# Other byte offsets for the on-chip arrays: the big region 128 bytes further, the split input activations 64 bytes further

## The chip, the core and the metric

The kernel runs on one core of one Trainium2 chip. Its time is device time in microseconds (us), the median of several executions; lower is better. On-chip memory (SBUF) has 128 partitions; an array that the kernel places there occupies the same byte offset in every partition, and this case is about those offsets alone. TensorE multiplies a stationary block of 128 columns, which a weight load (LDWEIGHTS) puts into the array first, by a moving block of up to 512 columns (MATMUL). Both blocks are read from SBUF.

## The reference

```python
h = rms_norm(x, norm_mix);  proj = h @ w_in          # 256 x 2048 by 2048 x 4624
out_a = sliding-window attention with sinks (16 heads, 4 key heads, rotary)
out_b = forgetting attention (16 heads)
x = x + concat(out_a, out_b) @ w_o                   # 2048 x 2048
h = rms_norm(x, norm_ffn)
u = h @ w_up                                         # 2048 x 11264
c = causal depthwise convolution of width 3 of u;  gate, val = halves of c
x = x + (silu(gate) * val) @ w_down                  # 5632 x 2048
return rms_norm(x, norm_final)
```

All is float32, for 256 tokens and one layer.

## The kernel before

Every large product is made of three. A float32 operand is split into a rounded part `hi` and a remainder `lo`, and the kernel adds hi·hi, hi·lo and lo·hi. ScalarE rounds (`split_hi`, L480; `down_hi`, L737), VectorE subtracts (`split_lo`, L793; `down_lo`, L1071), each a tile of 128 x 1024 at a time. SyncE loads the weight tiles of 512 KB into a ring of four slots, `raw`, and waits before each for `lo_done`; the halves go to the ring `split`.

The stages, in order of time:

- The first tiles (`values_and_gates`): activations `act_split` stationary, weights moving, 272 columns, three matmuls for each product (`mm3`, L1245 to L1247).
- Four passes of `quad`, for a head group each: `features` (L1257 and L1259: weights stationary, `act_split` moving, one matmul of 512 columns over hi and lo of the activations and one of 256), `tokens` (L1272 and L1274: `act_split` stationary, weights moving, 512 and 256), with the attention of the pass before between the tiles.
- The product with `w_o`: `mm3` with `mix_hi` and `mix_lo` stationary, weights of 512 columns moving.
- 22 `up_step`s (L1505 and L1507, in the form of `features`). Ahead of the first step's fourth tile stand four small matmuls on the array `diag2` (L1516), which spread the second norm's factors.
- The product with `w_down`: `mm3` with `g_hi` and `g_lo` stationary, 512 columns moving. Some tiles ("sums", one recursion of a fast product) use sums of activations instead, `s_hi` and `s_lo`, which lie in the space of `act_split`. VectorE also forms sums of weights (L1111 to L1116) for these.
- The last norm and the stores.

The arrays are placed one behind the other by a cursor. `Sbuf` starts it at the first free byte rounded up to 64, here 16512, and `place` rounds each size up to 32:

```python
        t = self.nc.alloc_sbuf_tensor_at(name, shape, dt, offset=self.cursor)
        self.cursor += (4 * int(np.prod(shape[1:])) + 31) // 32 * 32
```

A slot of the rings takes 4352 bytes, which is 8 · 512 + 256, so that neighbouring slots differ by 256 modulo 512. The offsets below are worked out from these two lines and the shapes; "modulo 512" is the offset's remainder.

| array | byte offset | modulo 512 |
|---|---|---|
| `raw`, `split` (slots 0 and 2; 1 and 3) | 16512, 33920 | 128; 384 |
| `nat` | 68736 | 128 |
| `act_split` (also `s_hi`, `s_lo`, `z_gain`) | 85120 | 128 |
| `ident`, `ones`, `cst`, `r2b`, `small` | 117888 to 121472 | 128; `small` 128 |
| region: `g_hi`, `g_lo`; in the same space `mix_hi`, `mix_lo` and the arrays of the attention | from 121856 | 0 |
| `ub`, `gfin` behind the region | 211968 | 0 |
| `conv_o`, `silu`, `up_r` | 216096 to 222240 | 32 |
| `diag2`, in the same space `t24` | 224288 | 32 |

Within an array the blocks that TensorE takes as stationary lie 512 bytes apart, so they keep the remainder. The moving blocks do too, except those of 272 columns: they lie 1088 bytes apart, 64 more modulo 512 for each next one.

Of the kernel before, what the change touches and what calls it, by code (L numbers as in the profile page):

```python
# [148 lines left out]
class Sbuf:  # L149


    def __init__(self, nc):
        self.nc, self.cursor = nc, (nc.sbuf_base + 63) // 64 * 64

    def place(self, name, shape, dt=F32):
        t = self.nc.alloc_sbuf_tensor_at(name, shape, dt, offset=self.cursor)
        self.cursor += (4 * int(np.prod(shape[1:])) + 31) // 32 * 32
        return t


def program(nc, x, norm_mix, w_in, sinks, b_f, w_o, norm_ffn, w_up, conv_w, conv_b, w_down, norm_final,
            ident_c, tri_c, mask_b_c, cos_c, sin_c, out):
    ctx = ExitStack()
    with ctx:
        sbuf = Sbuf(nc)
# [10 lines left out]
        split = sb("split", [P, 2, RING, SLOT], R32)  # L176
        hi, lo = split[:, 0], split[:, 1]
        nat = sb("nat", [P, MT, D])
        act_at = sbuf.cursor
        act_split = sb("act_split", [P, 2, KB, S], R32)  # L180
        act_hi, act_lo = act_split[:, 0], act_split[:, 1]
# [5 lines left out]
        small = sb("small", [P, 96])  # L187


        region = sbuf.cursor  # L190
        g_hi = sb("g_hi", [P, FB, S], R32)
        g_lo = sb("g_lo", [P, FB, S], R32)
# [43 lines left out]
        conv_o = sb("conv_o", [P, 2, 2, S])  # L236
        silu = sb("silu", [P, 2, S])
        up_r = sb("up_r", [P, 2, S])
        top = sbuf.cursor
        sbuf.cursor = region_end  # L240
        ysq = sb("ysq", [P, MT, 512])
# [1391 lines left out]
```

## Time and profile before

| | |
|---|---|
| median of 3 runs | 1074.91 us (1074.58 to 1075.35) |
| the profiled execution | 1073.68 us, span of its instructions 1071.9 us |
| granted TensorE clock | 0.999 of full speed |
| PE (matmuls) busy | 1060.3 us, 99% of the span |
| VectorE (DVE) busy | 803.3 us, 75% |
| ScalarE (ACT) busy | 614.1 us, 57% |
| DMA | 201.65 MB, mean 188 GB/s |

The profile has one record for each instruction. A matmul's duration in it is modelled and overlaps the next one's; what a matmul costs in a stream is read from the distance between two starts. Times in the timeline are rounded to 0.01 us, so distances are taken over several matmuls.

### The profile page before, as it was taken

How to read it: one execution, taken by the hardware profiler on the slowest of the kernel's cores; microseconds unless marked ns; L12 is line 12 of the kernel's file. 1: busy time of each engine (PE TensorE's matmuls, PEld its weight loads, DVE VectorE, ACT ScalarE, POOL GpSimd, SP SyncE). 2: the span in 40 equal slices, each digit the busy share in tenths (PEclk: the TensorE clock that was granted, in tenths of full speed). 3: DMA queues.
4: the chain of work that ended last, by engine and by line, in shares of the span. 5: the costliest groups of instructions: out<-in, count | busy, mean ns of one | idle time of the engine just before them, and what ended most of it. 6: DMA issues, size and time to landing. Idle time of an engine off the chain costs nothing.

```text
span 1071.9 us, 17534 instructions
## 1 busy us (share of the span) xinstructions
PE 1060.3 (99%) x5963; PEld 908.7 (85%) x5963; DVE 803.3 (75%) x1193; ACT 614.1 (57%) x946; POOL 9.5 (1%) x30
## 2 busy tenths in 40 slices
PE   9999999999999999999999999999999999999997
PEld 8888888888888888888888888888888788888885
DVE  5677777676565777877777777777877998887786
ACT  6957475745555655565555565555555555555553
POOL 1000000000000000000000000000000000000000
PEclk9999999999999999999999999999999999999999
DMA  9575556554555566556666566655666656556663
GB/s 298 170 235 173 174 164 176 158 175 154 180 171 183 174 199 195 181 172 202 192 197 188 167 206 191 199 180 175 199 194 194 201 193 204 189 194 202 202 198 127
DMA packets 171330, 201.65 MB, mean 188 GB/s; under 512 B 8580, under 2 KB 138340, under 8 KB 171168
## 3 DMA queue, kind: packets, MB, share of 16 engines
q1 hardware_dynamic: 170576, 199.59, 59.7%
q0 software_dynamic: 400, 1.27, 0.4%
q8 instruction: 21, 0.34, 0.1%
q10 hardware_dynamic: 320, 0.34, 0.1%
q14 instruction: 13, 0.11, 0.0%
HBM read 199.06 MB, written 2.11 MB: 188 GB/s over the span
## 4 chain that ended last, share of the span: by engine, by line
PE 97%; DVE 1%; DMA 1%; issue 0%; ACT 0%; SPq 0%; DVEq 0%; ACTq 0%
PE tr_ps L1505 15%; PE pj L1505 15%; PE pj L1257 9%; PE pj L1507 8%; PE tr_ps L1507 8%; PE pj L1245 5%; PE pj L1247 5%; PE pj L1246 5%; PE pj L1259 5%; PE sc_ps L1245 4%; PE sc_ps L1246 4%; PE sc_ps L1247 4%; PE pj L1272 3%; PE pj L1274 1%; PE tr_ps L1245 1%; PE tr_ps L1247 1%
## 5 line engine op out<-in xcount | busy, mean ns | idle before, releaser
L793 DVE TENSOR_TENSOR split<-raw,split 128x1024 fp32r<-128x1024 f32 x282 | 340.9, 1223 | 147.8 <-ACT split L480 142.3
L480 ACT ACTIVATE split<-raw 128x1024 fp32r<-128x1024 f32 x276 | 287.4, 1056 | 107.1 <-PE pj L1507 33.0
L1505 PE MATMUL tr_ps<-act_split,split 128*128 128x512 f32 x704 | 245.3, 391 | 0.0
L1505 PE MATMUL pj<-act_split,split 128*128 128x512 f32 x704 | 245.0, 391 | 0.0
L1507 PE MATMUL pj<-act_split,split 128*128 128x256 f32 x704 | 197.1, 280 | 0.0
L1507 PE MATMUL tr_ps<-act_split,split 128*128 128x256 f32 x704 | 197.1, 280 | 0.0
L1505 PEld LDWEIGHTS pj<-act_split,split 128*128 128x128 f32 x704 | 131.6, 187 | 28.9
L1505 PEld LDWEIGHTS tr_ps<-act_split,split 128*128 128x128 f32 x704 | 131.7, 187 | 28.8
L1257 PE MATMUL pj<-act_split,split 128*128 128x512 f32 x416 | 147.9, 399 | 0.0
L1507 PEld LDWEIGHTS tr_ps<-act_split,split 128*128 128x128 f32 x704 | 133.0, 189 | 0.1
L1507 PEld LDWEIGHTS pj<-act_split,split 128*128 128x128 f32 x704 | 133.1, 189 | 0.0
L1259 PE MATMUL pj<-act_split,split 128*128 128x256 f32 x416 | 116.1, 279 | 0.0
L737 ACT ACTIVATE split<-raw 128x1024 fp32r<-128x1024 f32 (+1 forms) x84 | 80.5, 984 | 34.9 <-PE sc_ps L1247 14.2
L1071 DVE TENSOR_TENSOR split<-raw,split 128x1024 fp32r<-128x1024 f32 (+1 forms) x84 | 92.2, 1131 | 4.1 <-ACT split L737 4.1
L1257 PEld LDWEIGHTS pj<-act_split,split 128*128 128x128 f32 x416 | 78.1, 188 | 18.4 <-issue 0.5
L1259 PEld LDWEIGHTS pj<-act_split,split 128*128 128x128 f32 x416 | 78.4, 188 | 0.0
L701 ACT ACTIVATE conv_o<-ub,cst 128x256 f32<-128x256 f32 x88 | 48.2, 596 | 22.2 <-DVE ub L1033 22.2
L1245 PE MATMUL sc_ps<-split,g_hi 128*128 128x512 f32 x148 | 58.6, 396 | 0.0
L1246 PE MATMUL sc_ps<-split,g_hi 128*128 128x512 f32 x148 | 58.4, 395 | 0.0
L1247 PE MATMUL sc_ps<-split,g_lo 128*128 128x512 f32 x148 | 58.4, 395 | 0.0
L737 ACT ACTIVATE split<-t 128x1024 fp32r<-128x1024 f32 x28 | 29.6, 1060 | 48.3 <-PE sc_ps L1247 27.5
L711 ACT ACTIVATE g_hi<-silu 128x256 f32 (+1 forms) x44 | 16.6, 418 | 54.7 <-DVE silu L1050 54.7
(244 smaller groups left out, 1502.5 us busy)
## 6 DMA issues: line engine op xcount, KB each, us to landing
raw<-w_up SPq DMA_DIRECT2D x176, 512.0 KB, 4.3
raw<-w_down SPq DMA_DIRECT2D x88, 512.0 KB, 4.4
raw<-w_in SPq DMA_DIRECT2D x72, 512.0 KB, 3.8
raw<-w_o SPq DMA_DIRECT2D x32, 512.0 KB, 4.3
nat<-x SPq DMA_DIRECT2D x8, 256.0 KB, 6.4
key_bias<-nft_dram SPq DMA_DIRECT2D x4, 512.0 KB, 4.8
result<-nat SPq DMA_DIRECT2D x7, 256.0 KB, 3.1
gfin<-norm_final POOLq DMA_DIRECT2D x1, 1024.0 KB, 4.8
```

Of the source, the lines that this page charges most:

```text
L480: act.activation(hi[:, slot, 0:TILE], raw[:, slot, 0:TILE], ACT.Copy).then_inc(hi_done, 1)
L701: act.activation(conv_o[:, v, b], ub[:, v, b, 2:S + 2], ACT.Identity, scale=tap(2, i * 2 + (b + v * FB)), bias=tap(3, i * 2 + (b + v * FB) ...
L737: act.activation(hi[:, slot, c0:TILE], down_source(t)[:, c0:TILE], ACT.Copy).then_inc(hi_done, 1)
L793: dve.tensor_tensor(lo[:, slot, 0:n], raw[:, slot, 0:n], hi[:, slot, 0:n].bitcast(F32), ALU.subtract).then_inc(lo_done, 1)
L1071: dve.tensor_tensor(lo[:, slot, c0:TILE], down_source(t)[:, c0:TILE], hi[:, slot, c0:TILE].bitcast(F32), ALU.subtract).then_inc(lo_done, 1)
L1245: pe.matmul(dst, a_hi, b_hi, start=start, stop=False, skip_group_check=True)
L1246: pe.matmul(dst, a_hi, b_lo, start=False, stop=False, skip_group_check=True)
L1247: return pe.matmul(dst, a_lo, b_hi, start=False, stop=True, skip_group_check=True)
L1257: pe.matmul(bank.rearrange("p (a n) -> p a n", a=2), wh[:, c, b * P:(b + 1) * P], act_split[:, :, k, :], start=first and c == 0, stop=Fals ...
L1259: ins = pe.matmul(bank[:, 0:S], wl[:, c, b * P:(b + 1) * P], act_hi[:, k], start=False, stop=True, skip_group_check=True)
L1505: pe.matmul(up_banks[v][b].rearrange("p (a n) -> p a n", a=2), wh[:, c, b * P:(b + 1) * P], act_split[:, :, k, :], start=k == 0, stop=Fals ...
L1507: ins = pe.matmul(up_banks[v][b][:, 0:S], wl[:, c, b * P:(b + 1) * P], act_hi[:, k], start=False, stop=True, skip_group_check=True)
```

## The change

`Sbuf` gets a function that moves the cursor forward to a given remainder modulo 512, and it is called at three places: ahead of `act_split`, ahead of the region, and ahead of `diag2` and `t24`.

```diff
+    def offset(self, remainder):
+
+        self.cursor += (remainder - self.cursor) % 512
+
...
         nat = sb("nat", [P, MT, D])
+        sbuf.offset(192)
         act_at = sbuf.cursor
         act_split = sb("act_split", [P, 2, KB, S], R32)
...
         small = sb("small", [P, 96])
 
 
+        sbuf.offset(128)
         region = sbuf.cursor
         g_hi = sb("g_hi", [P, FB, S], R32)
...
         up_r = sb("up_r", [P, 2, S])
+        sbuf.offset(32)
         top = sbuf.cursor
```

By the same reckoning `act_split` moves from remainder 128 to 192 (and with it `s_hi`, `s_lo`, `z_gain`, `ident`, `ones`, `cst`, `r2b`, `small`), everything in and behind the region moves by 128 bytes (`g_hi`, `g_lo`, `mix_hi`, `mix_lo` from 0 to 128), and `diag2` with `t24` moves by 512 bytes, so that it stays at 32. `raw`, `split` and `nat` don't move. No instruction, wait, transfer or order is added, removed or altered.

## Rows read from the trace of the kernel before

**Rows 1.** The page, busy time, share of the span and instructions by engine.
```profile
PE 1060.3 (99%) x5963; PEld 908.7 (85%) x5963; DVE 803.3 (75%) x1193; ACT 614.1 (57%) x946; POOL 9.5 (1%) x30
```

**Rows 2.** The page, chain that ended last, by engine.
```profile
PE 97%; DVE 1%; DMA 1%; issue 0%; ACT 0%; SPq 0%; DVEq 0%; ACTq 0%
```

**Rows 3.** Windows: us, PE, PEld, DVE, ACT, POOL busy (instructions), clock, DMA share, GB/s.
```profile
338.00:828.00 490.00, 490.00 (x2832) 432.13 (x2831) 376.74 (x615) 283.72 (x427) 0.00 (x0) 1.00 0.61 188
828.00:1064.00 236.00, 234.45 (x1011) 189.97 (x1010) 199.77 (x252) 124.62 (x145) 0.55 (x1) 1.00 0.58 190
```

**Rows 4.** Timeline of PE, a "sums" tile: start us, duration us, instruction.
```profile
858.04 0.39 PE L1246 MATMUL pj<-split,s_hi 128*128 128x512 f32 x1
...
860.31 0.40 PE L1247 MATMUL pj<-split,s_lo 128*128 128x512 f32 x1
```

**Rows 5.** Timeline of PE, a plain tile of the down stage.
```profile
940.46 0.39 PE L1245 MATMUL pj<-split,g_hi 128*128 128x512 f32 x1
...
943.25 0.40 PE L1245 MATMUL pj<-split,g_hi 128*128 128x512 f32 x1
```

**Rows 6.** Timeline of PE in the product with w_o.
```profile
285.12 0.39 PE L1245 MATMUL pj<-split,mix_hi 128*128 128x512 f32 x1
...
287.92 0.39 PE L1245 MATMUL pj<-split,mix_hi 128*128 128x512 f32 x1
```

**Rows 7.** Groups by form: matmuls, count, busy us, modelled mean ns, idle before.
```profile
L1505 PE MATMUL tr_ps<-act_split,split 128*128 128x512 f32 x704 | 245.3, 391 | 0.0
L1505 PE MATMUL pj<-act_split,split 128*128 128x512 f32 x704 | 245.0, 391 | 0.0
...
L1257 PE MATMUL pj<-act_split,split 128*128 128x512 f32 x416 | 147.9, 399 | 0.0
...
L1245 PE MATMUL sc_ps<-split,g_hi 128*128 128x512 f32 x148 | 58.6, 396 | 0.0
...
L1245 PE MATMUL pj<-split,g_hi 128*128 128x512 f32 x120 | 47.3, 394 | 0.0
L1272 PE MATMUL pj<-split,act_split 128*128 128x512 f32 x128 | 45.8, 400 | 0.0
...
L1245 PE MATMUL sc_ps<-split,mix_hi 128*128 128x512 f32 x64 | 25.7, 401 | 0.0
L1245 PE MATMUL pj<-split,mix_hi 128*128 128x512 f32 x64 | 25.4, 397 | 0.0
...
L1245 PE MATMUL pj<-split,s_hi 128*128 128x512 f32 x42 | 16.4, 389 | 0.0
...
L1245 PE MATMUL tr_ps<-split,g_hi 128*128 128x512 f32 x14 | 5.6, 397 | 1.5 <-DVE split L1071 1.5
```

**Rows 8.** Timeline of PE at the first sums tile of the down stage.
```profile
840.08 0.47 PE L1245 MATMUL tr_ps<-split,g_hi 128*128 128x512 f32 x1 [1.55 <-DVE split L1071]
```

**Rows 9.** Timeline of PE in the up stage.
```profile
500.31 0.39 PE L1505 MATMUL tr_ps<-act_split,split 128*128 128x512 f32 x1
...
505.51 0.39 PE L1505 MATMUL pj<-act_split,split 128*128 128x512 f32 x1
```

**Rows 10.** Timeline of PE in the second quad pass.
```profile
121.72 0.40 PE L1257 MATMUL pj<-act_split,split 128*128 128x512 f32 x1
...
124.54 0.40 PE L1272 MATMUL pj<-split,act_split 128*128 128x512 f32 x1
```

**Rows 11.** Timeline of PE in one of the first tiles, first matmul of blocks.
```profile
16.07 0.29 PE L1245 MATMUL pj<-split,act_split 128*128 128x272 f32 x1
...
16.83 0.29 PE L1245 MATMUL pj<-split,act_split 128*128 128x272 f32 x1
...
17.58 0.29 PE L1245 MATMUL pj<-split,act_split 128*128 128x272 f32 x1
...
19.09 0.38 PE L1232 MATMUL sc_ps<-ident,nat 128*128 128x128 f32 x2
```

**Rows 12.** Timeline of PE, restart of the stream in the first up step.
```profile
346.98 0.60 PE L1516 MATMUL pj<-diag,ones 128*128 128x128 f32 x4
```

## The prediction

> **What bounds the kernel.** I read the busy times first: TensorE's matmuls cover 99% of the span, VectorE 75% [rows 1]. The chain that ended last says the same in another way: 97% of it is TensorE [rows 2]. The windows by stage show that this holds in both long stages: no idle PE in the up stage, and 1.55 us in the down stage [rows 3], which is one wait for VectorE at the first sums tile [rows 8]. So the time is the number of matmuls times the distance between their starts, plus some 8 us behind the last one (1071.9 less 1064, where the window ends). The change adds and removes no instruction. It can act only through that distance, or through durations on other engines, and those have slack. The profiled execution took 1073.68 us, 1.23 us less than the median of 1074.91; I take differences from the trace and apply them to the median.
>
> **Does the distance depend on where the operands lie?** This trace can answer in part, because it has the same instruction (`mm3`, 128 stationary columns, 512 moving) with operands at different remainders.
>
> - Sums tiles, stationary blocks from `s_hi`, `s_lo`, remainder 128; moving blocks from `split` at 128 or 384. From the start at 858.04 to that at 860.31 lie 10 distances: 2.27 us / 10 = 227 ns [rows 4].
> - Plain tiles, stationary from `g_hi`, `g_lo`, remainder 0; the same moving ring. 12 distances take 943.25 − 940.46 = 2.79 us, 232.5 ns each [rows 5].
> - The product with `w_o`, stationary from `mix_hi`, `mix_lo`, remainder 0: 12 distances in 2.80 us, 233.3 ns [rows 6].
>
> The modelled means order the forms alike: 389 ns for `s_hi`, 394 to 401 for `g_hi` and `mix_hi` [rows 7]. The difference is 5.5 ns by rows 4 and 5. The two kinds alternate within one stage, partly on the same banks and beside the same work of VectorE and ScalarE, so I hold the offset for the cause and not the neighbours.
>
> **Edit 1, the region from 0 to 128.** After it the stationary blocks of the down stage and of the `w_o` product have the remainder that those of rows 4 have now, against the same moving blocks.
> Down stage: 148 + 120 + 14 = 282 products of three matmuls, 846 in all [rows 7]. At the first sums tile TensorE waits for VectorE [rows 8]; whatever it gains ahead of that it waits longer there. I leave out five tiles of 12 for this, 60 matmuls. (846 − 60) · 5.5 ns = 4.3 us.
> `w_o` product: (64 + 64) · 3 = 384 matmuls [rows 7], 384 · (233.3 − 227) = 2.4 us.
> Sum: 6.7 us. Bounds: at least nothing, if rows 4 are fast for another reason; at most what the whole distance above pure streaming could give: 512 columns at 2.4 GHz (granted clock 1.00 [rows 3]) take 213.3 ns, so (232.5 − 213.3) · 1230 = 24 us. I take 6.7, since a row shows precisely that configuration.
> Cover: VectorE is busy 199.77 of 236 us in the down stage [rows 3]. If TensorE needs 4.3 us less it is 86%, still not the bound. If that cover were gone in the sums tiles, where VectorE also forms four sums of weights, the wait of rows 8 would come back at each of the 14 groups; at up to the saved 5.5 ns · 60 = 0.3 us each it would at most eat the 4.3 us.
>
> **Edit 2, the activations from 128 to 192.** This is the uncertain one, because it touches the most matmuls: 1408 pairs (512 and 256 columns) in the up stage, 416 + 128 pairs in the quads [rows 7]. Now a pair takes (505.51 − 500.31) / 15 = 346.7 ns in the up stage [rows 9], whether the slot is at 128 or 384. Pure streaming of 768 columns would be 320 ns. So even here 26.7 ns are lost, 13.3 a matmul, about the 13.7 that rows 4 lose (227 − 213.3). I read that as what is left when the offsets do no harm.
> What 64 bytes do, no matmul of this length shows. The nearest rows are those of 272 columns: stationary blocks at 128, moving blocks that step by 64 bytes. Six matmuls take 16.83 − 16.07 = 0.76 us with the moving block at 128, 0.75 at 192 (the up stage's offsets after the change), and 12 take 1.51 us at 256 and 320 [rows 11]. So all of these offsets cost the same within 0.01 us in six, 1.7 ns a matmul. I take nothing for this edit, and keep as bounds −1.7 and +1.7 ns for each of 2816 matmuls of the up stage, ±4.8 us, from the resolution of rows 11. A wider bound comes from a cadence, below.
>
> **Edit 3 and the rest.** `diag2` keeps its remainder, and the arrays of the attention move along with the region. VectorE's and ScalarE's operands change offsets as well; they are off the chain [rows 2] and cost nothing unless one grows by more than the quarter of the span in which VectorE is idle [rows 1]. The offsets of DMA targets `raw` and `nat` stay.
>
> Sum: −6.7 us on 1074.9, 1068.2.
>
> **What the skill says.** The trace separates 227 from 232.5 ns by offset alone [rows 4, 5]. The Trainium skill, page "TensorE: Matmul & The Clock Gate", section "Step-by-step: what each phase is for", says that loading the next weights takes no SBUF read bandwidth from the running matmul, since each has a read port of its own. Under that rule placement would change nothing, and the sum would be 0 instead of −6.7; the rows above speak against it, but not for every offset.
>
> **The rivals.**
>
> A. *The up stage falls into the slow cadence (the other side).* In the second quad pass the same pairs, with the same offsets, take (124.54 − 121.72) / 8 = 352.5 ns [rows 10], not 346.7. So something besides offsets, the phase in which the stream restarted, picks between two cadences, and it stays over both tiles that these rows span. The up stage restarts once, behind the small matmuls at 346.98 [rows 12], and runs without a wait from there. If at offset 64 it lands in the slow cadence, it costs 1408 · 5.8 = 8.2 us; with edit 1 that is +1.5, 1076.4. It decides from 6.7 us / 1408 = 4.8 ns a pair on; from 6.3 ns the kernel is slower by over 0.2%. If the quads' pairs all went slow too, at most 544 · 5.8 = 3.2 us come on top: 1079.6. For it: the cadence exists, and every offset of TensorE's pairs changes. Against: rows 11 show no harm at 64.
>
> B. *64 bytes off helps.* If some of the 13.3 ns a matmul is still a collision of the two reads, moving them apart may take it away. By rows 11's resolution 4.8 us in the up stage, and up to 1.6 us in the quads by removing half of their slow pairs: 1068.2 − 6.4 = 1061.8. For it: the quads' slow pairs show that offset 0 or 256 between the two isn't safe in every phase. Against: those of 272 columns gain nothing visible.
>
> C. *Nothing happens.* Rows 4 are fast because the sums tiles reuse blocks or have shorter runs, not for the offset: 1074.9. By the skill's rule above it is the expected case. Against: the plain tiles are all slow and the sums tiles all fast in the modelled means [rows 7], and the up stage, at 128 too, has the low remainder of 13.3 ns.
>
> **Chances.** Forecast 0.50, A 0.22, B 0.20, C 0.08. A measurement of this kernel can tell about 0.2%, 2.1 us, from no change. A's own spread runs from 1073 to 1082, about two thirds of it above 1077 or so; so slower 0.15, same 0.14 (C and the lower part of A), faster 0.71. The range: B's low end leaves 0.1 below 1060, and the upper part of A leaves 0.1 above 1078. The forecast's own range is 1065 to 1071.
>
> **What would show it.** Right: in the down stage the starts of plain `mm3` matmuls 227 ns apart in place of 232.5, the same in the `w_o` product, so 12 matmuls in 2.72 us and the down window about 4 us shorter, and the up stage's 15 pairs still in 5.20 us. The forecast fails on its first step if `g_hi` matmuls stay at 232.5; on its second if 15 pairs in the up stage take more than 5.25 us or less than 5.15. A falls or stands by 8 pairs in 2.82 us within the up stage. If the sums tiles, whose stationary blocks go to 192, leave 227 ns, stationary offset and not only the difference to the ring matters. A new wait of PE for VectorE in a sums tile would show that the cover in the down stage is gone.

## The result, and the profile after

The changed kernel takes 1079.76 us (median of 6 runs, 1079.26 to 1080.0) against 1074.76 us for the kernel before in the same rounds: ratio 1.0046, 95% interval 1.0035 to 1.0056. It is slower by 5.0 us. The forecast was 1068.2 us with a range of 1060 to 1078; the time lies outside it, on the other side. In the experiments below one execution of e14_before_break_1 took 2168.01 us at a granted clock of 0.483; the ratio there leaves it out.

The page of the changed kernel shows what grew: PE, by 6.7 us, with the same 5963 matmuls and a granted clock of 0.998 (0.999 before).

```profile
span 1078.1 us, 17534 instructions
PE 1067.0 (99%) x5963; PEld 913.6 (85%) x5963; DVE 803.6 (75%) x1193; ACT 616.5 (57%) x946; POOL 9.5 (1%) x30
```

The timeline of PE in the changed kernel answers to [rows 4, 5, 6, 9]: in order of time the product with `w_o`, the up stage, a sums tile, and a plain tile of the down stage.

```profile
281.01 0.39 PE L1252 MATMUL pj<-split,mix_hi 128*128 128x512 f32 x1
...
283.73 0.39 PE L1252 MATMUL pj<-split,mix_hi 128*128 128x512 f32 x1
...
500.34 0.39 PE L1512 MATMUL tr_ps<-act_split,split 128*128 128x512 f32 x1
...
505.64 0.39 PE L1512 MATMUL tr_ps<-act_split,split 128*128 128x512 f32 x1
...
880.30 0.39 PE L1253 MATMUL pj<-split,s_hi 128*128 128x512 f32 x1
...
882.63 0.39 PE L1254 MATMUL pj<-split,s_lo 128*128 128x512 f32 x1
...
945.20 0.39 PE L1252 MATMUL pj<-split,g_hi 128*128 128x512 f32 x1
...
947.92 0.39 PE L1252 MATMUL pj<-split,g_hi 128*128 128x512 f32 x1
```

Twelve distances of `g_hi` and `g_lo` take 2.72 us, 226.7 ns each, where they took 2.79 [rows 5]. Twelve of `mix_hi` take 283.73 − 281.01 = 2.72 us instead of 2.80 [rows 6]. Ten of `s_hi` and `s_lo` take 2.33 us, 233 ns, where they took 2.27 [rows 4]. Fifteen pairs of the up stage take 505.64 − 500.34 = 5.30 us, 353.3 ns, where they took 5.20 [rows 9].

The instructions of one line show how long the up stage is, with the start of its first and last matmul of 512 columns. Of the kernel before:

```profile
L1505 PE MATMUL tr_ps<-act_split,split x704: 391/391/476, 337.8 to 815.8; 128*128 128x512 f32 x176
L1505 PE MATMUL pj<-act_split,split x704: 391/391/391, 350.2 to 826.9; 128*128 128x512 f32 x176
```

Of the changed kernel:

```profile
L1512 PE MATMUL tr_ps<-act_split,split x704: 388/397/475, 337.9 to 825.0; 128*128 128x512 f32 x176
L1512 PE MATMUL pj<-act_split,split x704: 392/397/398, 350.5 to 836.4; 128*128 128x512 f32 x176
```

This splits the 6.2 us by which the span of the profiled execution grew (the medians differ by 5.0; the profiled execution of the kernel before lies about 1 us below its median). Until the up stage begins, +0.1 us. The up stage, 489.1 to 498.5 us: +9.4. From its end to the end of the span, 1071.9 − 826.9 = 245.0 to 1078.1 − 836.4 = 241.7 us: −3.3. The +0.1 hides two changes, the `w_o` product faster by 1.9 us (96.6 to 94.7 us between its first matmul and the up stage's first), and what precedes it slower by 2.0: the first `features` matmul starts 0.7 us later (13.2 and 13.9 us), and the quads' pairs take 352.4 ns in place of 350.0, 1.2 us over the 513 that stand in an unbroken stretch. The 0.7 us can't be put down to the change: in the 16 traces that start lies anywhere from 13.0 to 14.3 us, whatever the offsets.

### The profile page after: what moved, and what is told of

Its sections match the earlier page's. It is cut to its first block, busy times and chain, and to the rows that moved or that the text cites. A ratio compares the mean times of both kernels' runs of the same rounds, so it can differ in the third digit from the quotient of the medians.

```text
span 1078.1 us, 17534 instructions
## 1 busy us (share of the span) xinstructions
PE 1067.0 (99%) x5963; PEld 913.6 (85%) x5963; DVE 803.6 (75%) x1193; ACT 616.5 (57%) x946; POOL 9.5 (1%) x30
## 4 chain that ended last, share of the span: by engine, by line
PE 98%; DVE 1%; DMA 0%; issue 0%; ACT 0%; DVEq 0%; SPq 0%; ACTq 0%
PE pj L1512 15%; PE tr_ps L1512 15%; PE pj L1264 9%; PE pj L1514 8%; PE tr_ps L1514 8%; PE pj L1253 5%; PE pj L1254 5%; PE pj L1252 5%; PE pj L1266 5%; PE sc_ps L1252 4%; PE sc_ps L1254 4%; PE sc_ps L1253 4%; PE pj L1279 3%; PE pj L1281 1%; PE tr_ps L1252 1%; PE tr_ps L1253 1%
## 5 line engine op out<-in xcount | busy, mean ns | idle before, releaser
L1512 PE MATMUL tr_ps<-act_split,split 128*128 128x512 f32 x704 | 249.9, 396 | 0.0
L1512 PE MATMUL pj<-act_split,split 128*128 128x512 f32 x704 | 249.7, 396 | 0.0
L1264 PE MATMUL pj<-act_split,split 128*128 128x512 f32 x416 | 149.0, 399 | 0.0
L744 ACT ACTIVATE split<-t 128x1024 fp32r<-128x1024 f32 x28 | 29.6, 1060 | 46.4 <-PE sc_ps L1254 26.7
```

Source lines behind the costliest of these rows:

```text
L744: act.activation(hi[:, slot, c0:TILE], down_source(t)[:, c0:TILE], ACT.Copy).then_inc(hi_done, 1)
L1264: pe.matmul(bank.rearrange("p (a n) -> p a n", a=2), wh[:, c, b * P:(b + 1) * P], act_split[:, :, k, :], start=first and c == 0, stop=Fals ...
L1512: pe.matmul(up_banks[v][b].rearrange("p (a n) -> p a n", a=2), wh[:, c, b * P:(b + 1) * P], act_split[:, :, k, :], start=k == 0, stop=Fals ...
```

## The experiments

The variants up to e7, and e10, are the changed kernel with other arguments of the function `offset`; e9 and e11 to e13 also change the small matmuls of the first up step, and e14 and e15 do the same to the kernel before. The diffs are against the kernel before; where one takes away a line `sbuf.offset(32)`, that line is the changed kernel's. "Distance" in the table is that between the starts of neighbouring matmuls, a mean over the trace without the places where the stream was broken. The theories' numbers stand in the expectations: theory 1, the distance of the stationary from the moving block modulo 256 bytes decides; theory 2, a block's own remainder decides; theory 3, the phase of a restart decides about the up stage.

| run | `act_split`, region, `diag2` (modulo 512) | us (median), ratio and interval to before | up pair, ns | `g`, `s` matmul, ns |
|---|---|---|---|---|
| before | 128, 0, 32 | 1074.7 to 1075.1 | 346.7 | 232.5, 227.9 |
| changed | 192, 128, 32 | 1079.76, 1.0046 [1.0035, 1.0056] | 353.3 | 227.2, 233.2 |
| e1_region_only | 128, 128, 32 | 1076.43, 1.0016 [1.0007, 1.0025] | 353.3 | 226.7, 226.9 |
| e2_act_only | 192, 0, 32 | 1086.12, 1.0104 [1.0089, 1.012] | 353.3 | 232.4, 232.7 |
| e3_act_384_region_384 | 384, 384, 32 | 1076.57, 1.0018 [1.0009, 1.0028] | 353.3 | 226.7, 226.9 |
| e4_act_256 | 256, 128, 32 | 1076.02, 1.0013 [1.0003, 1.0022] | 351.1 | 227.3, 233.0 |
| e5_region_256 | 128, 256, 32 | 1074.76, one execution | 346.7 | 232.5, 227.8 |
| e6_all_64 | 192, 192, 96, ring and `nat` at 192 too | 1075.88, one execution | 353.3 | 226.7, 226.7 |
| e7_region_diag_128 | 128, 128, 128 | 1075.92, 1.0013 [1.0004, 1.0023] | 353.3 | 226.7, 226.9 |
| e10_before_diag_128 | 128, 0, 128 | 1074.60, 1.0 [0.999, 1.0009] | 346.7 | 232.5, 228.2 |
| e9_third_small | as e1, diag2 matmul repeated | 1067.53, 0.9935 [0.9918, 0.9951] | 346.7 | 226.8, 226.8 |
| e11_break_after_3 | as e1, extra matmul after tile 4 | 1076.98, 1.0025 [1.0015, 1.0034] | 353.3 | 226.7, 226.8 |
| e12_break_after_1 | as e1, extra matmul after tile 2 | 1066.70, 0.9927 [0.9911, 0.9944] | 346.7 | 226.8, 227.3 |
| e13_changed_break_3 | as changed, extra matmul after tile 4 | 1080.38, one execution | 353.3 | 227.2, 233.2 |
| e14_before_break_1 | as before, extra matmul after tile 2 | 1075.08, 1.0002 [0.9992, 1.0012] | 346.7 | 232.5, 227.9 |
| e15_before_third_small | as before, diag2 matmul repeated | 1074.63, one execution | 346.7 | 232.5, 228.1 |

### Each edit alone

e1_region_only, the region moved and `act_split` back:

```diff
+        sbuf.offset(128)
         act_at = sbuf.cursor
...
+        sbuf.offset(128)
         region = sbuf.cursor
...
+        sbuf.offset(32)
         top = sbuf.cursor
```

> The region at 128 modulo 512, act_split left at 128, diag2 at 32. Theory 1 (the distance modulo 256 between the stationary and the moving block decides: 0 is good, 64 and 128 cost): g and mix matmuls of 512 columns 227 ns apart, up pairs 346.7 ns, s_hi matmuls 227 again; 1074.8 - 6.7 = 1068 us. Theory 2 (the remainder of a block by itself: stationary at 0 is bad, 128 and 384 good, 192 bad): the same numbers. Theory 3 (the up stage of the changed kernel was slow because its stream restarted in an unlucky phase, not because of the 64 bytes): the up pairs may be 353.3 ns here too, then about 1077 us.

Measured: 1076.43 us. The first edit gives what it should, 226.7 ns for the `g` matmuls and 227.4 for `mix`, and in the trace a down stage 4.8 us and a `w_o` product 1.9 us shorter, together the 6.7 that were forecast. But the up stage runs at 353.3 ns a pair although `act_split` lies where it lay in the kernel before. Theories 1 and 2 say 1068 and both miss by the whole up stage; theory 3 had named this outcome. The groups by form show both, `g_hi` now 389 instead of 396 and the up matmul 399 instead of 391 [rows 7]:

```profile
L1512 PE MATMUL tr_ps<-act_split,split 128*128 128x512 f32 x704 | 249.9, 399 | 0.0
...
L1252 PE MATMUL sc_ps<-split,g_hi 128*128 128x512 f32 x148 | 57.6, 389 | 0.0
```

e2_act_only, `act_split` at 192 and the region left:

```diff
+        sbuf.offset(192)
         act_at = sbuf.cursor
...
+        sbuf.offset(0)
         region = sbuf.cursor
...
+        sbuf.offset(32)
         top = sbuf.cursor
```

> act_split at 192, the region left at 0. Theories 1 and 2: up pairs 353.3 ns (1408 times 6.6 ns is 9.3 us more), g and mix matmuls at 232.5 ns as before, s_hi matmuls near 234; about 1074.8 + 9.3 + 1.1 plus what the quads lose, 1085 to 1087 us. Theory 3: up pairs 346.7 or 353.3 by chance; at 346.7 the time stays near 1075.

Measured: 1086.12 us, 11.3 us slower than before, as theories 1 and 2 say. e2 and the changed kernel differ only in the region, and that is worth 6.4 us. The two edits don't add up, though: alone they cost 1.6 and 11.3 us, together 5.0. With the up stage at 353.3 ns anyway, edit 1 brings its full gain; with `act_split` left alone it costs the up stage more than that.

### Which distances are good

e3 and e4 put `act_split` 256 and 128 bytes from the remainder 128 (e3 moves the region to 384 as well):

```diff
+        sbuf.offset(384)    # e4: 256
         act_at = sbuf.cursor
...
+        sbuf.offset(384)    # e4: 128
         region = sbuf.cursor
...
+        sbuf.offset(32)
         top = sbuf.cursor
```

> act_split and the region both at 384 modulo 512, 256 bytes off the remainder 128. Theory 1 (distance modulo 256): up pairs 346.7 ns, g, mix and s matmuls 227 ns, 1068 us, as with both at 128. Theory 2 (each block's own remainder): up pairs move a block at 384 that was moved at 128, nothing says it stays at 346.7; g at 384 unknown. Theory 3: up pairs 346.7 or 353.3 by chance.

> act_split at 256 modulo 512, the region at 128. Theory 1: s_hi matmuls stand 128 modulo 256 from the ring, as g_hi did in the kernel before, so 232.5 ns apart, and the up pairs lose about as much, 350 to 358 ns, 1072 to 1084 us. Theory 2: s_hi at 256 has a remainder of its own, not tried yet; if only stationary 0 and 192 are bad it is 227 ns and the up pairs 346.7, 1068 us.

Measured: e3 1076.57 us, in every distance like e1: `g` and `s` matmuls at 226.7 and 226.9 ns. So 384 is as good as 128: either differs from the ring by a multiple of 256. e4: the `s` matmuls, now 128 off modulo 256, go from 226.9 to 233.0 ns, as theory 1 says and theory 2 didn't; the up pairs take 351.1 ns, a cadence of their own.

e5 puts the region at 256, e6 moves everything by 64:

```diff
+        sbuf.offset(192)    # e6 alone
         raw = sb("raw", [P, RING, SLOT])
...
+        sbuf.offset(128)    # e6: 192
         act_at = sbuf.cursor
...
+        sbuf.offset(256)    # e6: 192
         region = sbuf.cursor
...
+        sbuf.offset(32)     # e6: 96
         top = sbuf.cursor
```

> The region at 256 modulo 512, act_split at 128, diag2 at 32. Theory 1 (distance modulo 256 between stationary and moving block): g and mix matmuls 232.5 ns apart as with the region at 0. Theory 2 (a block's own remainder; stationary at 0 is bad): 227 ns, as at 128 and 384. Up pairs: 346.7 or 353.3 ns, whichever cadence the restart behind the diag2 matmuls picks.

> Every array 64 bytes further than in the run with the region alone at 128: ring, nat, act_split and region all at 192 (or 448), diag2 at 96. Theory 1 (only distances count): the same as that run, g, mix and s matmuls 226.7 ns, up pairs in the same cadence of 353.3 ns, about 1076.4 us. Theory 2 (a block's own remainder counts, 192 is bad): s, g and mix matmuls at 233 ns or more, about 1083 us.

Measured: e5 has `g` and `mix` matmuls at 232.5 ns, so a stationary block at 256 costs what one at 0 does. e6, with stationary blocks at 192 and the ring moved along, has 226.7 ns and the up pairs at 353.3, like e1; in the changed kernel a stationary block at 192 against the ring at 128 cost 233.2 (`s`). This pair settles the first edit: of the distances tried (0, 64 and 128 modulo 256) the distance between the stationary and the moving block counts, and a block's own remainder doesn't. Theory 2 falls. From e5, by form:

```profile
L1252 PE MATMUL sc_ps<-split,g_hi 128*128 128x512 f32 x148 | 58.6, 396 | 0.0
```

### What decides the up stage

e7 and e10 change only `diag2` (e7 against e1, e10 against the kernel before). The small matmuls ahead of the up stage's fourth tile read it, two in the source and four in the profile:

```diff
-        sbuf.offset(32)     # e7: region 128; e10: region 0; act_split 128 in both
+        sbuf.offset(128)
         top = sbuf.cursor
```

> The region at 128, act_split at 128, and diag2 at 128 in place of 32. Only the four small matmuls ahead of the up stage's fourth tile read it. Theory 3 (the restart picks the up stage's cadence): its start may shift by a few ns and the up stage may fall into 346.7 ns a pair; then 1408 times 6.6 ns less than with diag2 at 32, 1067 us. If it picks the same cadence, 1076.4 us. A theory in which offsets of the long operands alone decide the up stage says 353.3 ns and 1076.4 us.

> The kernel before with diag2 (and t24) at 128 in place of 32 and nothing else moved modulo 512. Theory 3: the up stage of the kernel before ran at 346.7 ns because its restart fell well; with another start of the small matmuls it may be 353.3 ns, 1074.8 + 9.3 = 1084 us, or unchanged at 1074.8. If diag2 has no say in the cadence: 1074.8.

Measured: e7 1075.92 us, the up stage as slow as in e1; e10 1074.60 us, as fast as in the kernel before. The remainder of `diag2`, which the change took care to keep, has no say here. Theory 3 isn't touched: both runs restart as their sisters do.

So the next runs leave every offset of e1 as it is and change the break itself. e9 repeats the first small matmul, e11 and e12 add one whose result nobody reads:

```diff
-                        for m in range(MT):
+                        for m in (0, 0, 1):                       # e9
                             pe.wait_ge(diag2_s, m + 1)
...
+                    if first and s == 1:                          # e12; e11: s == 3, bank 3
+                        pe.matmul(pj[:, 2, 0:P], ones[:], ones[:], start=True, stop=True)
```

> Offsets as in the run with the region alone at 128 (act_split 128, diag2 32). The first of the two small matmuls on diag2 is done twice, same result. Offsets identical, only the break ahead of the up stage's fourth tile is longer. Theory 3 (the restart picks the cadence): the up pairs may go to 346.7 ns, then about 1067 us, or stay at 353.3. Theories in which offsets decide the up stage: 353.3 ns and 1076.5 us.

> The run with the region alone at 128, and one more small matmul (ones by ones, into a free bank, its result unused) behind the first up step's fourth tile: one more restart while the stream is in the slow cadence. Theory 3: the cadence may switch, 346.7 ns a pair from there on, 1067 us; else 353.3 and 1076.5. Theories of offsets alone: 353.3, 1076.5.

> The run with the region alone at 128, and the same small unused matmul behind the first up step's second tile, ahead of the diag2 matmuls. The stream is in the fast cadence of 346.7 ns there. Theory 3, in its form that the cadence ahead of a restart decides the one behind it: the tile behind the extra matmul goes to the slow cadence and the diag2 matmuls restart it from there, so the up stage may end in the fast one, 1067 us. Else 353.3 and 1076.5.

Measured: e9 1067.53 us and e12 1066.70 us, with up pairs at 346.7 ns; e11 1076.98 us with 353.3. The same long instructions at the same offsets run the rest of the up stage in one cadence or in the other, and one small matmul near its start decides. But e12 didn't go the way that its expectation drew: the tile behind the extra matmul stayed fast, 344.75 − 342.67 = 2.08 us for 6 pairs, and the stream left the next restart fast too. So "fast or slow ahead of the break" isn't what decides. The timeline of e1 shows the switch at the restart. Ahead of the small matmuls 8 pairs take 344.82 − 342.05 = 2.77 us, 346 ns each; behind the restart 8 pairs take 348.79 − 345.96 = 2.83 us, 354 ns:

```profile
342.05 0.39 PE L1512 MATMUL tr_ps<-act_split,split 128*128 128x512 f32 x1
...
344.82 0.39 PE L1512 MATMUL tr_ps<-act_split,split 128*128 128x512 f32 x1
...
345.96 0.39 PE L1512 MATMUL tr_ps<-act_split,split 128*128 128x512 f32 x1
...
348.79 0.40 PE L1512 MATMUL pj<-act_split,split 128*128 128x512 f32 x1
```

(The small matmuls start at 345.17.) In e12, with the extra matmul at 342.10 and the small ones at 345.10, 8 pairs behind the same restart take 348.67 − 345.89 = 2.78 us:

```profile
342.67 0.40 PE L1512 MATMUL tr_ps<-act_split,split 128*128 128x512 f32 x1
...
344.75 0.40 PE L1512 MATMUL tr_ps<-act_split,split 128*128 128x512 f32 x1
...
345.89 0.40 PE L1512 MATMUL tr_ps<-act_split,split 128*128 128x512 f32 x1
...
348.67 0.39 PE L1512 MATMUL pj<-act_split,split 128*128 128x512 f32 x1
```

e13 asks whether the changed kernel, 64 bytes off, has a fast cadence as well; its edit is that of e11 on the changed kernel.

> The changed kernel itself (act_split at 192, 64 off the ring) with the small unused matmul behind the first up step's fourth tile. If at a distance of 64 there is no fast cadence, the up pairs stay at 353.3 ns through this restart too, 1079.8 us; if it was only unlucky, they may go to 346.7, 1070 us.

Measured: 1080.38 us, 353.3 ns a pair ahead of the extra restart and behind it. The changed kernel, e2 and e13 together passed the restart behind the y transposes (eight small matmuls behind the first tile), the one behind `diag2` and one more, and came to 353.3 ns each time. That is no proof that no break leads elsewhere. A faster cadence at 64 does exist, in the same trace of the changed kernel: from 44.4 to 71.7 us, early in the quads, 78 pairs run at 349 ns (15 pairs from 65.38 to 70.61 take 5.23 us). It isn't 346.7, which no stretch of the three traces at a distance of 64 reaches.

e14 and e15 put the breaks of e12 and e9 into the kernel before.

> The kernel before, offsets untouched, with the small unused matmul behind the first up step's second tile that took the region-alone version to 1066.7 us. If the fast cadence of the kernel before hangs on its restart, as theory 3 says, the same extra matmul may take it away: up pairs 353.3 ns, 1074.9 + 9.3 = 1084 us. If the extra matmul is good in itself: no slower than 1075. If the kernel before keeps 346.7 ns the theory isn't refuted, since both cadences are allowed.

> The kernel before, offsets untouched, with the first of the two small diag2 matmuls done twice, which took the region-alone version to 1067.5 us. Theory 3: up pairs 346.7 ns (about 1075 us) or 353.3 ns (1084 us) by the restart alone; a look at the first tile behind the restart says which, and whether it stays.

Measured: 1075.08 and 1074.63 us, up pairs at 346.7 ns in both. The extra matmul is worth nothing where the up stage is fast already, so in e12 it is the cadence that it buys. And e14 has, between its extra matmul and the `diag2` restart, one tile in the slow cadence, at the old offsets: six pairs take 347.11 − 344.99 = 2.12 us, 353 ns each; behind the restart six take 350.33 − 348.25 = 2.08 us, 347 ns (the extra matmul starts at 344.42):

```profile
344.99 0.40 PE L1505 MATMUL tr_ps<-act_split,split 128*128 128x512 f32 x1
...
347.11 0.40 PE L1505 MATMUL tr_ps<-act_split,split 128*128 128x512 f32 x1
...
348.25 0.40 PE L1505 MATMUL tr_ps<-act_split,split 128*128 128x512 f32 x1
...
350.33 0.40 PE L1505 MATMUL tr_ps<-act_split,split 128*128 128x512 f32 x1
```

The kernel before thus had the slow cadence within reach of its up stage too, and its two restarts there happened to end in the fast one.

The means hide what does decide. The traces keep the starts in ns, and pair by pair they show a repeating pattern:

| distance modulo 256 | pairs in order, ns | mean |
|---|---|---|
| 0, "even" | 347, 347, 346 | 346.7 |
| 0, "alternating" | 350, 343 | 346.7 |
| 0, "slow" | 349, 350, 361 | 353.3 |
| 64, in the up stage | 348, 357, 355 | 353.3 |
| 64, in the stretch at 349 ns | 351, 349, 347 | 349.0 |
| 128 (e4) | 346, 354, 353 | 351.1 |

So the 353.3 ns of the changed kernel and those of e1 are two patterns with one mean. And at a distance of 0 all 12 traces, one execution of each kernel, fit one list of what a break in the first up step makes of the pattern ahead of it:

| break | ahead, behind | runs |
|---|---|---|
| y transposes | even, alternating | before, e5, e10, e14, e15 |
| | slow, even | e1, e3, e6, e7, e9, e11, e12 |
| `diag2` matmuls | alternating, even | before, e5, e10, e12 |
| | even, slow | e1, e3, e6, e7, e11 |
| | slow, alternating | e14 |
| the same, first one repeated | even, even; alternating, even | e9; e15 |
| extra small matmul | even, alternating; alternating, slow; slow, slow | e12; e14; e11 |

The first tile is even wherever the `w_o` product ran at 232.5 ns and slow wherever it ran at 227.4. That is the way by which edit 1 alone reaches the up stage: it starts it in another pattern, and the same two breaks then end in another one. The list was read from the traces afterwards; no run was made to test it.

## Why the prediction was wrong

**Edit 1** was right in mechanism and size. In steady stretches the `g` and `mix` matmuls went to 226.7 ns (227 forecast), and e1, where nothing else moves, gave the forecast 6.7 us in these two stages. The sum said −4.3 us for the down stage and −2.4 for `w_o`. In the changed kernel the `w_o` product gave −1.9: its mean between the broken places went from 232.5 to 227.6 ns, since [rows 6], at 233.3, had shown 12 that were dearer than most, and since the first matmuls behind each break still take up to 236; a mean over the stage was the better row. The down stage gave −3.3: −4.5 from 841 `g` matmuls at 5.3 ns, given back in part by edit 2, which moved `s_hi` and `s_lo` 64 bytes off the ring and cost 166 · 5.3 ns = 0.9, and by the wait at the first sums tile, which grew as foreseen, from 1.55 [rows 8] to 1.79:

```profile
849.57 0.47 PE L1252 MATMUL tr_ps<-split,g_hi 128*128 128x512 f32 x1 [1.79 <-DVE split L1078]
```

The sum had left the `s` matmuls out. The prediction also said that sums tiles leaving 227 ns would show the stationary offset to matter by itself; they did leave it, but their distance to the ring changed with it, and e6 shows that it was the distance.

**Edit 2** is the step that failed. It was taken at nothing, with ±1.7 ns a matmul, because six matmuls of 272 columns cost alike at 128 and 192 [rows 11]. The up stage paid 6.6 ns a pair, 9.4 us, and e2, with this edit alone, is 11.3 us slower than the kernel before. Rows of 272 columns didn't carry over to matmuls of 512 and 256: their mean distance was 125.5 ns before and 125.1 in the changed kernel, so they show no cost of this edit even now. Why they don't, no run shows; their own moving blocks step by 64 bytes every six matmuls, so that the stream never keeps one distance for long. The `s` matmuls, 512 columns, would have told (227.9 to 233.2 ns), but only after the change.

A second term stood at nothing without being named: what edit 1 does to the up stage. In e1 it is +9.2 us, more than the 6.7 that the edit gains, so the forecast of 1068.2 would have failed without edit 2 as well, at 1076.4.

**Edit 3** was rightly taken at nothing: e7 and e10 give the remainder of `diag2` no say, and VectorE's busy time went from 803.3 [rows 1] to 803.6 us.

**Rival A** is what happened, in size: 353.3 ns a pair in place of 346.7 (352.5 had been read from [rows 10]), and its 8.2 us were 9.4. Its mechanism, the restart, is shown to exist by e1, e9 and e12, at the distance of 0 modulo 256. In the changed kernel it is another thing: the pattern there is that of the distance 64, not the slow one of [rows 10], and it came behind every restart tried in the up stage, so the match in size is in part luck. The offset cost the changed kernel its up stage, and e1 shows that without this offset, with `diag2` as it is, the restart would have cost it anyway. The prediction also counted one restart in the up stage [rows 12]; there are two, the y transposes behind the first tile being the other. The rival got 0.22; it deserved more, since the kernel before showed the slow cadence in its quads, and edit 1 changes the stretch ahead of the up stage, which sets the pattern that the breaks start from.

**Rival B** fell: 64 bytes helped neither the up stage nor the `s` matmuls nor the quads as a whole. The quads' pairs went from 350.0 to 352.4 ns a pair.

**Rival C** fell: e1 took the plain tiles to 226.7 ns and e4 the sums tiles to 233.0 with their order and blocks unchanged, and e5 and e6 tie the 5.8 ns to the distance. The Trainium skill, page "TensorE: Matmul & The Clock Gate", section "Step-by-step: what each phase is for", has the weight load take no read bandwidth from the running matmul. As the prediction read it, placement then changes nothing; 226.7, 232.5 and 233 ns for one instruction at three distances disagree with that, and the measurement decides. That the two reads collide is the obvious reading, but no run here shows the collision itself.

**The range** ended at 1078, 0.1 of chance above it; rival A at 6.6 ns a pair with the quads' loss and the `s` matmuls gives 1068.2 + 9.3 + 1.2 + 0.9 = 1079.6, near the measured 1079.76, so its upper part was priced too low.

**What stays open**: why a break turns one pattern into the next. Among the runs at distance 0 the times repeat from execution to execution, and the outcome goes with the pattern ahead of the break and with the break (e1 and e9 differ by one repeated small matmul), but no run explains the patterns. The version that beats both kernels is e12, 1066.70 us, 0.73% faster than before: in its trace the down stage is 4.6 us shorter than in the kernel before, the `w_o` product 1.9 and the quads 0.8.

## What to carry to other kernels

Where TensorE is the bound, compare the distance between matmul starts for the same form at different operand offsets, and put stationary and moving blocks at a multiple of 256 bytes from one another: one line of placement was worth 6 us here, in the stages that it was meant for. Then check after any edit, however unrelated, that the long loop is still in its fast cadence, by timing 15 matmuls of one line in the timeline; if it isn't, a small extra matmul ahead of the loop may bring it back (those of e9 and e12 did, that of e11 didn't; the up stage of e12 is 0.3 us longer than that of the kernel before, for 9 us gained over e1). Don't price an offset by rows of another length.

## What was unexpected about the hardware

- A matmul of 512 columns behind a weight load takes 226.7 ns from start to start when stationary and moving blocks start a multiple of 256 bytes apart, 232.5 at 128, 233 at 64. Moved together by 64 bytes, they cost nothing (e6).
- A stream of pairs of 512 and 256 columns has two stable speeds at the same offsets, 346.7 and 353.3 ns, which it keeps for 480 us without a wait. A break of a few hundred ns picks, by the pattern (three of them at distance 0) that the stream had ahead of it.
- The mean alone can mislead: 353.3 ns stands for a pattern of 349, 350, 361 at distance 0 and for one of 348, 357, 355 at distance 64.
